# Even mixer of a two-block network on one core: root spreads, mask and scores from halves

## The reference, cut to what matters

```python
def even_mixer(h_lat, h_ctx, ...):
    qa, ka, va, qb, kb, vb = heads(h_lat)          # h @ w_in, rms_norm over each head's 64
    qa_c, ka_c, va_c, qb_c, kb_c, vb_c = heads(h_ctx)
    qa, ka = rope_2d(qa, row, col), rope_2d(ka, row, col)
    o_a = window_attention(qa, ka, va, ka_c, va_c, a_sink)   # local scores + mask |q-k| <= 128, ctx, sink
    o_b = neighbourhood_attention(qb, kb, vb, kb_c, vb_c, b_rpb, rows_n)  # local scores + bias, ctx
    y_lat = concat([o_a, o_b]) @ w_out
    # the context tokens attend to themselves in the same way, without mask, rope or bias
```

## Time and profile before

| | us |
|---|---|
| median of 3 runs | 2181.19 (2176.37 to 2184.78) |
| the profiled execution | 2178.84 |
| its span | 2177.2 |
| TensorE busy | 2101.7 (97%) |
| VectorE busy | 1535.6 (71%) |
| ScalarE busy | 911.1 (42%) |

### The profile page before, as it was taken

One profiled execution on the slowest core, in us unless ns is written; L12 is line 12 of the kernel. 1 busy time (PEld: TensorE's weight loads), 2 busy tenths in 40 slices (PEclk: granted clock), 3 DMA queues, 4 the chain that ended last, 5 costly groups with the idle time before them and its releaser, 6 DMA issues.

```text
span 2177.2 us, 37792 instructions
## 1 busy us (share of the span) xinstructions
PE 2101.7 (97%) x14330; PEld 1776.7 (82%) x14330; DVE 1535.6 (71%) x2584; ACT 911.1 (42%) x1516; POOL 30.0 (1%) x60
## 2 busy tenths in 40 slices
PE   7999999999999999999999999999999999999998
PEld 6889988889889998889975676788887875559987
DVE  7776768776887677887744556767787566667854
ACT  5554645554565443565422434312111233344332
POOL 0000000000000000000000000000000000000000
PEclk9999999999999999999999999999999999999999
DMA  7665515665554632455611110324445522003453
GB/s 280 246 228 179 201 62 213 256 227 187 191 190 166 224 136 98 153 190 181 218 59 39 40 40 20 143 97 153 176 173 196 199 89 97 1 23 133 179 185 137
DMA packets 50514, 326.71 MB, mean 150 GB/s; under 512 B 5361, under 2 KB 8689, under 8 KB 17265
## 3 DMA queue, kind: packets, MB, share of 16 engines
q1 hardware_dynamic: 42480, 266.62, 34.1%
q0 software_dynamic: 7936, 58.76, 7.2%
HBM read 324.30 MB, written 1.05 MB: 149 GB/s over the span
## 4 chain that ended last, share of the span: by engine, by line
PE 82%; DVE 10%; ACT 4%; issue 3%; DVEq 0%; DMA 0%; ACTq 0%; SPq 0%
PE psum L2074 14%; PE psum L2019 9%; PE psum L2021 8%; PE psum L2020 8%; PE psum L2075 7%; PE psum L2131 4%; PE psum L2132 4%; PE psum L2133 4%; PE psum L2628 3%; DVE w_lo L1119 2%; PE psum L2467 2%; PE psum L2629 1%; ACT scratch L918 1%; ACT w_hi L651 1%; PE psum L2152 1%
## 5 line engine op out<-in xcount | busy, mean ns | idle before, releaser
L651 ACT ACTIVATE w_hi<-raw 128x1024 fp32r<-128x1024 f32 (+1 forms) x542 | 515.3, 992 | 599.7 <-PE psum L2021 353.3
L1119 DVE TENSOR_TENSOR w_lo<-raw,w_hi 128x1024 fp32r<-128x1024 f32 (+1 forms) x534 | 589.5, 1145 | 152.2 <-ACT w_hi L651 138.5
L2074 PE MATMUL psum<-h_both,w_hi 128*128 128x512 f32 x1344 | 475.5, 398 | 4.1 <-DVE rope_tmp L1169 2.7
L2075 PE MATMUL psum<-h_both,w_lo 128*128 128x256 f32 x1344 | 377.3, 281 | 0.0
L2074 PEld LDWEIGHTS psum<-h_both,w_hi 128*128 128x128 f32 x1344 | 252.6, 188 | 65.5 <-DVE w_lo L1119 3.0
L2019 PE MATMUL psum<-h_both,w_hi 128*128 128x256 f32 (+1 forms) x792 | 255.9, 323 | 6.4 <-DVE h_both L1588 1.9
L2075 PEld LDWEIGHTS psum<-h_both,w_lo 128*128 128x128 f32 x1344 | 254.6, 189 | 0.0
L2020 PE MATMUL psum<-h_both,w_hi 128*128 128x256 f32 (+1 forms) x792 | 252.4, 319 | 0.0
L2021 PE MATMUL psum<-h_both,w_lo 128*128 128x256 f32 (+1 forms) x792 | 252.3, 319 | 0.0
L2131 PE MATMUL psum<-g_both,w_hi 128*128 128x256 f32 x704 | 201.8, 287 | 1.2 <-DVE w_lo L1119 1.2
L2132 PE MATMUL psum<-g_both,w_hi 128*128 128x256 f32 x704 | 199.1, 283 | 0.0
(11 more groups left out here) (374 smaller groups left out, 3592.3 us busy)
## 6 DMA issues: line engine op xcount, KB each, us to landing
raw<-in_weights SPq DMA_DIRECT2D x207, 1024.0 KB, 4.8
raw_ada<-in_ada POOLq DMA_DIRECT2D x48, 1024.0 KB, 5.1
raw<-in_weights SPq DMA_DIRECT2D x64, 704.0 KB, 4.1
arena<-in_rpb POOLq DMA_DIRECT2D x1, 2048.0 KB, 11.4
arena<-in_fox_c POOLq DMA_DIRECT2D x1, 1696.0 KB, 8.9
const_region<-in_latent_c POOLq DMA_DIRECT2D x1, 1394.0 KB, 6.2
const_region<-in_even_c POOLq DMA_DIRECT2D x1, 1360.0 KB, 8.9
x_res<-in_x_lat SPq DMA_DIRECT2D x4, 256.0 KB, 6.7
```

Source lines behind the costliest of these rows:

```text
L651: nc.scalar.activation(wh[s][:, a], raw[s][:, a], ACT.Copy).then_inc(hi_ready, 1)
L1119: V.tensor_tensor(wl[s][:, a], raw[s][:, a], wh[s][:, a].bitcast(F32), ALU.subtract).then_inc(lo_ready, 1)
L2074: mm(psum[:, o, :], w_hi, h_both[:, :, k, 0:T], start=k == 0, stop=False)
L2075: ins = mm(psum[:, o, 0:T], w_lo, hh[:, k, 0:T], start=False, stop=k == DC - 1)
```

## The change

Three parts, all in the even mixer.

1. Spreads. After a root, VectorE writes the reciprocals of 64 rows to PSUM, copies them as high halves to `e_row_r` and writes the low halves (a subtraction) into rows 32 to 63. The sum tables place each head's sum twice, in rows r and r + 32, and the spread tables are doubled likewise, so a spread is one F32R product over 64 rows. ScalarE copies the spread table to F32R once, before the first square.
2. Mask. ScalarE copies mask and identity to F32R once; the mask of the window heads is added with one F32R product. The bias of the other heads stays F32.
3. Scores. ScalarE copies each chunk's high half after its rotation (chunks 0 to 4) or its spread (5 to 12), VectorE subtracts its low half in new steps "low" and inside slots 1, 4, 6, 14, 15, 16, 18 and 19 (between `step_shift` and `step_weigh`), and all scores are three F32R products. TensorE waits at each pair's first slot for the low halves.

In the order, "low" 4 and 0 come after "spread" 1; "spread" 5 and 9 move from behind unit 16 to ahead of it, and "low" 5 and 9 stand behind it. Buffers move so that two of them have F32R views. The diff, without the allocations and tables:

```diff
@@ even_order
             yield "spread", 1
+            yield "low", 4
+            yield "low", 0
...
             yield "root", 1
             yield from unit(15)
-            yield from unit(16)
             yield "spread", 5
             yield "spread", 9
+            yield from unit(16)
+            yield "low", 5
+            yield "low", 9
             yield "slot", 12
...
+        E_LOW_IN = {1: (1,), 4: (2,), 6: (3,), 14: (6, 10), 15: (7,), 16: (11,), 18: (8,), 19: (12,)}
@@ scalar, even
                     elif what == "sum":
+                        if k == 0:
+                            act.wait_ge(phase_loaded[2], 32)
+                            tell(sel_made, creg_r[0:64, e_bsel_cols], creg[0:64, e_bsel_cols], ACT.Copy)
                         act.wait_ge(bank_free, unit_of[k + (k >= 5)] + 3)
...
+                        if k == 0:
+                            act.wait_ge(phase_loaded[2], 32)
+                            tell(mask_made, w_mask_r[:], w_mask, ACT.Copy)
+                            tell(mask_made, ident_r[:], ident, ACT.Copy)
...
-                        nc.scalar.activation(e_row[0:rows, :], psum[0:rows, 7, :], ACT.Sqrt,
-                                             bias=small[0:rows, 40:41]).then_inc(e_rooted, 1)
+                        nc.scalar.activation(e_row[0:64, :], psum[0:64, 7, :], ACT.Sqrt,
+                                             bias=small[0:64, 40:41]).then_inc(e_rooted, 1)
                     elif what in ("spread", "rope"):
                         pos.u += 1
                         pos.e += 1
+                        if what == "rope" or k > 4:
+                            if what == "rope":
+                                act.wait_ge(e_roped, (k + 1) % 5 + 1)
+                            else:
+                                act.wait_ge(bank_free, pos.u + 2)
+                            tell(e_hi_made, e_high(k), e_qk[:, k, :], ACT.Copy)
@@ vector
+            def stack_halves(row, row_r, turn):
+                step(V.reciprocal(turn, row[0:64, :]))
+                step(V.tensor_copy(row_r[0:64, :], turn))
+                V.tensor_tensor(row_r[32:64, :], turn[32:64, :], row_r[32:64, :].bitcast(F32),
+                                ALU.subtract).then_inc(e_row_done, 1)
...
                     step_shift(k)
+                    if not first:
+                        for key in E_LOW_IN.get(k, ()):
+                            even_low(key)
                     step_weigh(k)
+
+            def even_low(k):
+                dve.wait_ge(e_hi_made, E_HI.index(k) + 1)
+                V.tensor_tensor(e_qk_lo[:, k, :], e_qk[:, k, :], e_high(k).bitcast(F32), ALU.subtract).then_inc(e_lo_made, 1)
...
                     elif what == "root":
-                        rows = (10, 16)[k]
                         dve.wait_ge(e_rooted, k + 1)
-                        V.reciprocal(e_row[0:rows, :], e_row[0:rows, :]).then_inc(e_row_done, 1)
+                        stack_halves(e_row, e_row_r, psum[0:64, 7, :])
@@ tensor, step_scores
+                pairs = ((e_high(q), e_high(key)), (e_high(q), e_qk_lo[:, key, :]), (e_qk_lo[:, q, :], e_high(key)))
                 for t in sorted({job[1] for job in s["jobs"]}):
-                    for m in range(2):
-                        r = slice(64 * m, 64 * m + 64)
-                        col = 0 if base == 0 else t * T
-                        ins = mm(psum[:, 2 + m, col:col + L], e_qk[r, q, base + t * P:base + (t + 1) * P],
-                                 e_qk[r, key, TJ - L:TJ], start=True, stop=base != 0)
+                    col = 0 if base == 0 else t * T
+                    for n, (qs, ks) in enumerate(pairs):
+                        for m in range(2):
+                            r = slice(64 * m, 64 * m + 64)
+                            ins = mm(psum[:, 2 + m, col:col + L], qs[r, base + t * P:base + (t + 1) * P], ks[r, TJ - L:TJ],
+                                     start=n == 0, stop=base != 0 and n == 2)
...
-                        bias = w_mask[:, t, :] if s["kind"] == "a" else b_bias[:, t, 2 * c + m, :]
-                        ins = mm(psum[:, 2 + m, 0:T], ident, bias, start=False, stop=True)
+                        if s["kind"] == "a":
+                            ins = mm(psum[:, 2 + m, 0:T], ident_r[:], w_mask_r[:, t, :], start=False, stop=True)
+                        else:
+                            ins = mm(psum[:, 2 + m, 0:T], ident, b_bias[:, t, 2 * c + m, :], start=False, stop=True)
@@ tensor, even
-                        mm(psum[0:group, 7, :], e_sel[:, k, 0:group], e_sq[:, k % 2, :], start=k == first,
+                        mm(psum[0:64, 7, :], e_sel_of(k), e_sq[:, k % 2, :], start=k == first,
                            stop=k == last).then_inc(e_sq_used, 1)
...
-                        mm(out, e_bsel[0:rows, k, :], e_row[0:rows, :], start=True, stop=True).then_inc(gemm_done, 1)
+                        mm(out, e_bsel_r[0:64, k, :], e_row_r[0:64, :], start=True, stop=True).then_inc(gemm_done, 1)
...
-                        if k in (0, 3, 6, 9):
-                            pe.wait_ge(e_roped, k // 3 + 2)
...
+                        if k % 3 == 0 and k < N_EVEN_STEPS:
+                            c = k // 3
+                            needs = (c, 4) if c < 4 else (1 + c, 5 + c)
+                            pe.wait_ge(e_lo_made, 1 + max(E_LOW.index(n) for n in needs))
```

More of the change, by code:

```diff
@@ L62 @@
 FFN_FIRST, UP = 3, 4
+SEL_W = 78
+LSEL_W = SEL_W + 92 + 3 * 64
 def weight_plan():
@@ L98, in build @@
         ada_part = sb("ada_part", [P, 64])
-        n_blk = sb("norm_blk", [P, 6 * T])
+        ARENA = 4 * 16384
+        at = int(nc.sbuf_usable_end) // 64 * 64 - ARENA - 64
+        raw_at = at - 4 * SLOT
+        creg_at = raw_at - 4 * 2800
+        blk_at = creg_at - 4 * 6 * T
+        n_blk = nc.alloc_sbuf_tensor_at("norm_blk", [P, 6 * T], F32, offset=blk_at)
+        n_blk_r = nc.alloc_sbuf_tensor_at("norm_blk_r", [P, 6 * T], F32R, offset=blk_at)
         n_sq = n_blk[:, 0:TJ].rearrange("p (a b) -> p a b", a=2)
@@ L183, in build @@
         cc = Carve(creg)
-        e_sel, e_bsel, cos_a, sin_a, rot_a = cc(13, 32), cc(13, P), cc(T), cc(T), cc(P)
+        e_sel, e_bsel, cos_a, sin_a, rot_a = cc(SEL_W), cc(13, P), cc(T), cc(T), cc(P)
         NCE = cc.n
+        e_bsel_cols = slice(SEL_W, SEL_W + 13 * P)
+        e_bsel_r = creg_r[:, e_bsel_cols].rearrange("p (a b) -> p a b", a=13)
+        e_row_r = n_blk_r[:, 2 * TJ:3 * TJ]
+        e_at = lambda k: k if k < 5 else k - 5
+        e_sel_of = lambda k: e_sel[:, 14 - 2 * e_at(k):78 - 2 * e_at(k)]
         cm = Carve(arena)
@@ L491, in even_order, with e_high @@
                 yield "out", q
+        E_LOW_IN = {1: (1,), 4: (2,), 6: (3,), 14: (6, 10), 15: (7,), 16: (11,), 18: (8,), 19: (12,)}
+        E_HI = [k for what, k in even_order() if what == "spread" and k > 4 or what == "rope"]
+        E_LOW = [k for what, k in even_order() if what == "low" and k < 5]
+        E_LOW += [k for n in (1, 4, 6) for k in E_LOW_IN[n]] + [5, 9]
+        E_LOW += [k for n in (14, 15, 16, 18, 19) for k in E_LOW_IN[n]]
+        def e_high(k):
+            if k < 4:
+                return ya_hi[:, k, :]
+            if k == 4:
+                return ya_lo[:, 3, :]
+            if k in (5, 9):
+                return n_blk_r[:, TJ * (k == 9):TJ * (k == 9) + TJ]
+            return hh[:, k - 1, :] if k < 9 else hl[:, k - 5, :]
         LAT_SIDE = {("cq", 2): 2, ("kv", 0): 4}
@@ L1816, in even @@
                         pos.e += 1
+                    elif what == "low":
+                        even_low(k)
                     elif what == "slot":
@@ L2547, in even @@
                         if k == 5:
-                            pe.wait_ge(e_rooted, 1)
-                        group, first, last = (10, 0, 4) if k < 5 else (16, 5, 12)
+                            pe.wait_ge(e_row_done, 1)
+                        first, last = (0, 4) if k < 5 else (5, 12)
                         pe.wait_ge(e_sq_made, k + 1)
-                        mm(psum[0:group, 7, :], e_sel[:, k, 0:group], e_sq[:, k % 2, :], start=k == first,
+                        mm(psum[0:64, 7, :], e_sel_of(k), e_sq[:, k % 2, :], start=k == first,
                            stop=k == last).then_inc(e_sq_used, 1)
                     elif what == "spread":
-                        rows = 10 if k < 5 else 16
+                        pe.wait_ge(sel_made, 1)
                         rope_after[k] = pos.u + 3
@@ L2980, in _arrays @@
     out["sb_c"] = _join(np.concatenate([m0, m1], axis=1), tri, -np.ones((P, P)))
-    sel, bsel = np.zeros((P, 13, 32), np.float32), np.zeros((32, 13, P), np.float32)
+    bsel = np.zeros((32, 13, P), np.float32)
     for first, n in ((0, 5), (5, 8)):
-        sel[:, first:first + n], bsel[:, first:first + n] = _head_tables(n, 32)
+        bsel[:, first:first + n] = _head_tables(n, 32)[1]
+    sel = np.zeros((P, SEL_W), np.float32)
+    for half in range(2):
```

(4 more changed lines are left out.)

23 lines of the change are left out of this document (12 added, 11 removed).

## The result

The changed kernel takes 2190.23 us as a median of 12 executions (2181.43 to 2193.39); the kernel before, run beside it, 2181.88 (12 executions, 2176.37 to 2188.88). The ratio is 1.0039, with a 95% interval of 1.0026 to 1.0052. Run once more later, as g4_again, the same kernel took 2183.03 (ratio 1.0014, 0.9995 to 1.0032). So the change does not gain the 8 us that I forecast. By the first run it costs 8 us; by the second 1.6 us in the medians and 3 us in the ratio, whose interval also holds no change at all. 2190 lies just above my range (2161 to 2189); 2183 would lie in it, but by the clock and not by my sum.

The account below looks back on a forecast made before the run. TensorE, busy 97% of the span, was taken to bound the kernel. Terms of 3.0 - 2.5 - 7.7 + 4.6 - 5.4 = -8.0 us gave a median of 2173 us, range 2161 to 2189.

Parts of the forecast that it names:

- sum 6: At the mixer's start: its product waits for ScalarE's square behind chunk 4's copy, an idle of 3.8 us.
- rival C: Score products: half products in 64-row tiles run one after another, a pair 0.48 us; 2188 us in all, chance 0.15.
- the fifth chunk's spread: At the second root: the spread waits 2.1 us for the copy and subtraction that follow the reciprocal.
- step 12: Behind the second root: its start waits about 2 us for VectorE's low half.
- The second root: Between steps 11 and 12: waits add 2.9 us and a slow clock stretch 1.7, +4.6 in all.
- -2.5 + 3.0: Mixer's start: scores of step 0 done 3.0 us later, then steps 0 to 2 take 2.5 us less.
- my 7.7: Steps 3 to 11, taken as TensorE-bound: shorter masks, scores and one spread take off 7.7 us.
- so no new wait opens: Steps 12 to 23: the chain to the exponentials starts earlier by the scores' saving, so 5.4 us come off.
- in its waits for the turns: Steps 3 to 11: ScalarE's 0.64 us copies are covered by its waits; without cover a step would lose 0.7 us.
- half of one such 3.4 us stretch: Half clock behind a new gap, at the start and again at the second root: 1.7 us added each time.
- rival D: Steps 3 to 23: more idle brings four more 3.4 us half-clock stretches, costing 6.8 us; 2180 us, chance 0.15.
- A's stall: The forecast case: overlapped halves save time, with two new stalls, at start and second root; 2166 to 2180 us, chance 0.43.

Follow-up runs that it names:

- f1_noscore: The changed kernel with scores from F32 operands in the order of before, no chunk halves made; stacked spreads and half-product mask stay: 2174.39 us, ratio 0.9977.
- g2_spreads: The kernel before with the stacked spreads alone, mask and scores in full precision: 2182.2 us, ratio 1.0012.
- e3_act15: The changed kernel with ScalarE's copy of chunk 11's high half behind the next weight rounding instead of ahead of it: 2182.6 us, ratio 1.0002.
- e1_sum6: The changed kernel with ScalarE's copy of chunk 4's high half behind the square for "sum 6" instead of ahead: 2178.0 us, ratio 0.9981.
- e2_root: The changed kernel with the low halves of chunks 5 and 9 made ahead of unit 16 instead of behind it: 2186.9 us, ratio 1.0019.
- f2_pad4: The kernel before with four needless products between two dense layers behind the even mixer, to shift what follows: 2187.4 us, ratio 1.0024.
- f3_pad8: The kernel before with eight needless products between two dense layers behind the even mixer, to shift what follows: 2185.5 us, ratio 1.0020.
- e4_all: The changed kernel with all three moves, those of e1_sum6, e2_root and e3_act15: 2175.12 us, ratio 0.9968.
- g1_after_fill: The changed kernel, all waits kept, with 24 needless products on TensorE at six places where it idled: 2175.52 us, ratio 0.9976.

## Why the prediction was wrong, by its own steps

**Right.** Halves in 64-row tiles run side by side: in the timeline of step 0 the three pairs take 0.34, 0.24 and 0.32 us each to the next start, not 0.48, so rival C is out. The trace agrees with the Trainium skill ("TensorE: Matmul & The Clock Gate", Why this matters for your kernels), which has small-K products in distinct row groups run concurrently.

```profile
1161.95 0.50 PE L2516 MATMUL psum<-y_low,y_high 64*128 64x512 f32 x2
1162.29 0.40 PE L2516 MATMUL psum<-e_qk_low,y_high 64*128 64x512 f32 x2
1162.53 0.39 PE L2516 MATMUL psum<-y_low,e_qk_low 64*128 64x512 f32 x2
1162.85 0.51 PE L2521 MATMUL psum<-w_mask_r,ident_r 128*128 128x256 f32 x2
1163.19 0.40 PE L2601 MATMUL psum<-h_both,w_hi 128*128 128x512 f32 x1
```

The stalls that I worked out are there: "sum 6" idle 3.51 us (3.8 forecast), the fifth chunk's spread 2.33 (2.1), step 12 2.16 (2). The second root cost +4.6, as forecast, but 2.4 of it without the clock where I had 2.9; that the sum agrees to a tenth is luck. From the first spread to step 2 the change took off 0.9 where I had -2.5 + 3.0 = +0.5: the start took its half clock earlier (1153.7 instead of 1160.3), not more of it.

**Sizes of the terms.** A step's scores cost 0.90 us and not 0.78, and the mask 0.34 and not 0.24: the first pair of a group and the one ahead of the mask take 0.1 longer (0.34 and 0.32) than the pair between them (0.24). In 18 of the 24 steps the scores take 0.89 to 0.91. A step so saves 0.16 + 0.63 and not 0.28 + 0.73: 6 x 0.79 + 3 x 0.16 + 0.75 = 6.0 in steps 3 to 11. Two idles of TensorE there grew, from 0.34 to 0.96 us and from 0.65 to 0.80, so 5.2 of my 7.7; the segment has 4.8 at full clock.

**The step that failed: "so no new wait opens".** Steps 12 to 23 were to give 5.4 us; they took 2.3 more, and at full clock gave 0.6. I wrote for steps 12 to 23 that "the chain from scores to exponentials starts earlier by what the scores save", and for the copies that they lie "in its waits for the turns". The first forgets that ScalarE's order is strict: a copy which waits for VectorE holds the weight rounding behind it, and VectorE needs that rounding. That opened the new wait of 1.68 us at step 17, which before, f1_noscore and g2_spreads don't have; e3_act15 moved one copy, the wait went, and 2.2 us with it. With e1_sum6's and e2_root's orders mended too, steps 12 to 23 give 3.3 at full clock (77.0 to 73.7). With the measured 0.16 for the scores my term would be 12 x 0.16 + 2.0 = 3.9.

**The price that failed: half clock.** I counted "half of one such 3.4 us stretch" for the start and as much for the root, 3.4 in all, and gave 0.15 to rival D, which had four more stretches. The mixer had 13.6 us more at half clock than before had in its profile, four stretches of 3.4 us, just the number of D, and 20 to 27 more than f2_pad4 and f3_pad8 had. T x c and the clock show it over all executions: about 5 us less of work, 8 to 11 lost to the clock. D's number came true, its mechanism in part: of the four, two stand behind the waits for the exponentials at steps 18 and 21 (2.49 us where before had 1.27, and 2.33 where it had 2.16), one at the root, which is A's stall, and one behind an idle of 1.86 us that before has unchanged. Nor does the idle alone decide: that of 2.49 us is in g2_spreads, f1_noscore and e4_all too, without half clock behind it. I read one profile's stretches as a property of its gaps. Before's had more of them than f2_pad4's and f3_pad8's of the same code, so that the change had more clock to lose than my rows showed.

**Still open.** How much slower the changed kernel is (1.0039 or 1.0014), and what makes the two differ; which of the idles bring the half clock that the fill took away, since g1_after_fill filled six places at once; and what sets whether a given gap is followed by half clock.

## What to carry to other kernels

Where products are shortened between answers of other engines, the freed time turns into idle, and TensorE's clock may take back more than the work gave: count the gaps behind which dense work stands (those that half clock followed here were of 1.0 to 3.5 us), and fill them or remove their cause before judging the change. A copy put on a strictly ordered engine costs what its wait holds up behind it, not its own length. Judge an edit of a few us by time multiplied by granted clock, against the kernel before of the same batch, and by part: here a changed mask product alone gave as much at full clock as the whole change, and the largest part, the scores, cost more than it saved until its waits were mended.

## What the runs showed of the hardware

Idle stretches of TensorE of 1.64, 2.33 and 2.49 us were followed within 1.5 us by 3.4 or 6.8 us at 1.2 GHz, while after 1.68 us at 1310.03 and 2.16 at 1271.28 the clock stayed up. An idle of 2.48 or 2.49 us ahead of step 18 was followed by 3.4 us at 1.2 GHz in five profiles (changed, g4_again, e1_sum6, e2_root, e3_act15) and by full clock in three (g2_spreads, f1_noscore, e4_all). Identical code had 20.5, 13.7 and 6.8 us at half clock in the even mixer of three profiles, whereas two executions of the changed kernel (its own profile and g4_again's) had the same eight stretches, each at the same distance from step 0 to 0.1 us. With 24 needless products added, the changed kernel's median was 7.5 us lower (2183.03 to 2175.52). Two half products of 512 columns over 64 rows each cost 0.24 us together (1162.29 to 1162.53), as much as one over 128 rows (1149.07 to 1149.31 in the kernel before). A reciprocal of 512 columns took 3.34 us over 10 and over 16 partitions before, and 3.35 over 64 after.
